# One DMA instead of two to spread the relative-bias rows over 128 scratch lines

## The chip, the cores and the metric

The kernel runs on one core of a Trainium2 chip. The metric is device time in microseconds (us) of one execution, the median of several. The same program is launched once; nothing is computed on the host.

## The reference, cut to what matters

Two blocks run one after the other on 256 tokens of width 1024. The first has two layers: layer 0 with a gated linear attention beside a sparse attention, then a dense SwiGLU; layer 1 with a forgetting and a dilated attention, then eight SwiGLU experts. The second block has one layer with an attention, a convolution and a SwiGLU. Three of these attentions add a bias that depends only on the distance between query and key:

```python
# layer 0 (sparse attention), rel_table: (32 buckets, 8 heads)
bias = rel_table[_rel_bucket(tq[None, :, None] - sel)]
logits = logits + bias.transpose(0, 3, 1, 2).astype(jnp.float32)
# layer 1 (dilated attention)
bias = rel_table[_rel_bucket(offs)].T.astype(jnp.float32)
lg = (jnp.einsum('bqhd,bqjhd->bhqj', qb, ksel) * dh ** -0.5 + bias[None, :, None, :])
# second block, rel_bias: (32, 8)
s_own = s_own + bias_ht[:, t5_bucket(jnp.maximum(dist_own, 0))]
```

## The kernel before, in words

**The bias tables.** For each of the three attentions the kernel first makes one row per head: 8 heads (on 8 partitions) by 384 distances, so 1.5 KB per partition. PE makes it with a one-hot product (L828, L829) and ACT copies it from PSUM into `relrow`, which lies in the tile `u` (L1275). What the attention adds is a table of 128 queries by 8 heads by 256 keys in which each query's line is the row shifted by one place. The shift is made by addressing: the rows are written 128 times into a scratch tensor in DRAM (`rel_dram`, named `rel_scratch` in the profile, 3 x 128 x 8 x 384 floats, 1.5 MB for each attention), and `bias_table` (L1977 to L1980) reads that with a pitch that is one element short, so that partition t gets the row from place 127 - t on. Its result is the tile `bias` (1 MB).

**How the scratch is written before.** POOL first stores the three small rows to a DRAM tensor `rel_rows` (L2014, 12 KB each), waits until all three have landed (L2015), then issues three DRAM-to-DRAM DMAs that each write 128 copies (L2017), and then `bias_table(0)`, which waits for the first of the three alone. Later `bias_table(1)` and `bias_table(2)` wait for theirs.

**POOL's queue around it** is a fixed order: norm weights, the steps above, `bias_table(0)`, the `rstd` of the gated linear attention (L1985), and, when the first attention has given its result, `bias_table(1)`. A wait in this queue holds everything behind it.

**Who depends on it.** DVE waits on `rel_out`, counted to 48, at L1749, because the next instructions overwrite `u` (L1753); at L1761 it waits for `rel_in[0]`, the bias table of the first attention, before the first add at L1597.

**The weights.** SP streams all weights in units of 1 MB into a ring of six (L411). ACT rounds each unit to its upper part (L1130, `upper`), DVE forms the rest (L1500, `lower`), and the end of DVE's instruction frees the place in the ring, so SP issues the load for the unit that is used six units later. PE takes three products for each pair of tiles (L524, L526, L527). In layer 0 each unit of 256 columns is one projection of q, k, v and so on; the sparse attention (L612 to L644) is threaded between the last of them. All DMAs, SP's and POOL's, are served by the same 16 DMA engines; queue q1 in the profile is SP's, q0 is POOL's.

Of the kernel before, what the change touches and what calls it, by code (L numbers as in the profile page):

```python
# [18 lines left out]
F32 = mybir.dt.float32  # L19
# [7 lines left out]
P = 128  # L27
# [4 lines left out]
H = 8  # L32
# [11 lines left out]
REL = 384  # L44
# [66 lines left out]
def build(nc, x_in, ln_g, ln_b, rel_table, w_in_ab, w_gate_a, b_gate_a, g_norm_a, w_out_ab, w_in_cd,  # L111
# [5 lines left out]
    with ctx:  # L117
# [3 lines left out]
        def sem(name):  # L121
            return ctx.enter_context(nc.semaphore(name))
# [59 lines left out]
            return psum[:, 2 * (i % 2):2 * (i % 2) + 2, 0:n]  # L182


        rel_rows = nc.dram_tensor("rel_rows", (3, H, REL), F32, kind="Internal").ap()
        rel_dram = nc.dram_tensor("rel_scratch", (3, P, H, REL), F32, kind="Internal").ap()


# [2 lines left out]
        relrow = uf[0:8, 2 * REL:5 * REL].rearrange("p (a n) -> p a n", a=3)  # L191
# [73 lines left out]
        ln_in = sem("norm_weights")  # L265
        late_in = sem("late_constants")
        rel_out = sem("rel_rows_out")
        rel_spread = [sem(f"rel_rows_spread_{i}") for i in range(3)]
        rel_in = [sem(f"rel_bias_in_{i}") for i in range(3)]
        rel_ready = sem("rel_row_ready")  # L270
        tr_done = sem("transposed")
# [1202 lines left out]
        def _(dve):  # L1474
# [20 lines left out]
            def lower():  # L1495

                u_, _, i, n = halves.place()
                s_ = halves.s
                dve.wait_ge(hi_ready[s_], n + 1)
                dve.tensor_tensor(lower_half[i], ring[:, u_, :], upper_half[i].bitcast(F32), ALU.subtract)\  # L1500
                   .then_inc(taken[s_][u_], 1)
# [467 lines left out]
        @block.gpsimd  # L1969
        def _(pool):  # L1970
            def weights(n, rows):
                if n >= 1:
                    pool.wait_ge(x_ready, n)
                for i, r in enumerate(rows):
                    pool.dma_start(lnw[:, i, :], r.broadcast_to([P, D])).then_inc(ln_in, 16)

            def bias_table(i):  # L1977
                pool.wait_ge(rel_spread[i], 16)
                src = bass.AP(rel_dram.tensor, i * P * H * REL + P - 1, [[H * REL - 1, P], [REL, H], [1, T]])
                pool.dma_start(bias[:, :, :], src).then_inc(rel_in[i], 16)  # L1980

            def rstd_of(n):
                asked[0] += 1
                pool.wait_ge(rs_ask, asked[0])
                pool.tensor_tensor(rstd8[:, 0:n], e2[:, 0:n], half[:, 0:n], ALU.pow).then_inc(rs_got, 1)  # L1985

            def rstd_tiles():
                for t in range(TT):
                    asked[0] += 1
                    pool.wait_ge(rs_ask, asked[0])  # L1990
                    pool.tensor_tensor(rstd8[:, t:t + 1], e2[:, t:t + 1], half[:, 0:1], ALU.pow).then_inc(rs_got, 1)

            halves = Split()

            def lower(s_, n):

                halves.at(s_, n)
                u_, _, i, n = halves.place()
                pool.wait_ge(hi_ready[s_], n + 1)
                pool.tensor_tensor(lower_half[i], ring[:, u_, :], upper_half[i].bitcast(F32), ALU.subtract)\  # L2000
                    .then_inc(taken[s_][u_], 1)

            def link(ins):
                chain[0] += 1
                ins.then_inc(g_chain, 1)
                pool.wait_ge(g_chain, chain[0])

            chain = [0]
            asked = [0]
            weights(0, (ln_g[0, 0:1, :], ln_b[0, 0:1, :]))  # L2010

            for i in range(3):
                pool.wait_ge(step_evac, 7 + i)
                pool.dma_start(rel_rows[i], relrow[:, i, :]).then_inc(rel_out, 16)  # L2014
            pool.wait_ge(rel_out, 48)  # L2015
            for i in range(3):
                pool.dma_start(rel_dram[i], rel_rows[i].unsqueeze(0).broadcast_to([P, H, REL])).then_inc(rel_spread[i], 16)  # L2017
            bias_table(0)
            pool.wait_ge(filled, 3)
            rstd_of(8)  # L2020
            pool.wait_ge(a_done, 2)
            bias_table(1)
            lower(0, 18)
            rstd_tiles()
            weights(1, (ln_g[0, 1:2, :], ln_b[0, 1:2, :]))
            pool.dma_start(rowsel[:, :, :], c_rowsel).then_inc(late_in, 16)
            lower(0, 18 + 3 * NCH_D)
            rstd_tiles()
            weights(2, (ln_g[1, 0:1, :], ln_b[1, 0:1, :]))
            pool.wait_ge(a_done, 6)  # L2030
            bias_table(2)
            pool.wait_ge(late_in, 16)
            pool.dma_start(convw[0:31, :], conv_w_2[0]).then_inc(late_in, 16)
            pool.dma_start(convw[31:32, :], conv_b_2).then_inc(late_in, 16)
            pool.dma_start(convg[:, :], conv_ln_g_2.broadcast_to([P, 512])).then_inc(late_in, 16)
            pool.dma_start(convb[:, :], conv_ln_b_2.broadcast_to([P, 512])).then_inc(late_in, 16)
            lower(0, LENGTHS[0])
            rstd_tiles()
            weights(3, (ln_g[1, 1:2, :], ln_b[1, 1:2, :]))
            pool.dma_start(mixg, mix_norm_g_2.broadcast_to([P, D])).then_inc(ln_in, 16)  # L2040
            rstd_tiles()
            rstd_tiles()
            weights(5, (ffn_norm_g_2,))

            rstd_of(2)
            lower(1, 11)
            rstd_tiles()
            weights(6, (final_norm_g_2.rearrange("(a d) -> a d", a=1),))
            rstd_tiles()
# [57 lines left out]
```

## Time and profile before

| | us |
|---|---|
| median of 3 runs (lowest, highest) | 1989.35 (1987.8, 1989.61) |
| the profiled execution | 1987.8 |
| its span, first to last instruction | 1985.7 |
| PE busy | 1871.4 (94%) |
| DVE busy | 1373.9 (69%) |
| ACT busy | 1110.0 (56%) |
| POOL busy | 50.5 (3%) |
| DMA: moved, mean rate | 490.43 MB, 247 GB/s |

The profiled execution lasts 2.1 us longer than its span and is the fastest of the three. Times inside the trace count from the span's start. Nearly all of the span is the stream of expert weights through PE; the change concerns the first tenth of it, in which the rows are made at 44 us, the scratch is written until 69 us and the first attention runs from 130 to 184 us.

### The profile page before, as it was taken

To read this page: it belongs to the slowest core of one execution; us is meant where nothing else is said; L and a number is where in the kernel's file an instruction comes from. 1 tells how busy PE (TensorE), PEld (TensorE's weight loads), DVE (VectorE), ACT (ScalarE), POOL (GpSimd) and SP (SyncE) were. 2 spreads that over 40 slices of the span, in tenths; PEclk is the share of its full clock that TensorE was granted. 3 is DMA by queue.
4 is the path that set the end of the run, shared out by engine and by line. 5 is a ranking of instruction groups with operands and counts; after the bars stand their busy time and mean duration, and the time that the engine had idled before them with its cause. 6 is when DMAs were issued, how large, how long until landed. Compare 5 with 4: busy or idle time off the path is not lost.

```text
span 1985.7 us, 26183 instructions
## 1 busy us (share of the span) xinstructions
PE 1871.4 (94%) x10221; PEld 1590.4 (80%) x10221; DVE 1373.9 (69%) x1207; ACT 1110.0 (56%) x1031; POOL 50.5 (3%) x49
## 2 busy tenths in 40 slices
PE   6999899989979999999999999999999978779998
PEld 5896799968967878878888788787887858669997
DVE  3742545453467888888888788888888875955544
ACT  4532343443436767677777777777767743334343
POOL 0000100010020000000000000000000000010000
PEclk9996899988979999999999999999999988789999
DMA  9631555542357999999999899998999972324551
GB/s 283 223 128 43 171 185 179 186 149 86 123 173 258 371 323 355 347 324 373 337 338 369 308 369 343 334 370 312 359 342 336 370 265 79 124 64 163 187 190 43
DMA packets 252154, 490.43 MB, mean 247 GB/s; under 512 B 14178, under 2 KB 96651, under 8 KB 251716
## 3 DMA queue, kind: packets, MB, share of 16 engines
q1 hardware_dynamic: 248144, 474.74, 68.3%
q0 software_dynamic: 3184, 14.29, 2.1%
q8 instruction: 38, 0.62, 0.1%
q10 hardware_dynamic: 772, 0.65, 0.1%
q14 instruction: 16, 0.13, 0.0%
HBM read 488.56 MB, written 5.80 MB: 249 GB/s over the span
## 4 chain that ended last, share of the span: by engine, by line
PE 87%; DVE 8%; issue 2%; ACT 2%; SPq 1%; DMA 1%; POOLq 0%; DVEq 0%; POOL 0%; ACTq 0%
PE psum L524 26%; PE psum L526 25%; PE psum L527 25%; DVE ta L1937 2%; PE psum L965 2%; PE psum L1037 2%; PE psum L1011 1%; DVE wl L1500 1%; ACT wh L1130 1%; PE psum L585 1%; PE psum L670 1%; PE psum L644 1%; PE psum L612 1%; DVE u L1881 1%; PE psum L697 1%
## 5 line engine op out<-in xcount | busy, mean ns | idle before, releaser
L1500 DVE TENSOR_TENSOR wl<-ring,wh 128x2048 fp32r<-128x2048 f32 x446 | 1021.9, 2291 | 406.2 <-ACT wh L1130 405.8
L1130 ACT ACTIVATE wh<-ring 128x2048 fp32r<-128x2048 f32 x450 | 861.6, 1915 | 428.1 <-PE psum L524 354.9
L524 PE MATMUL psum<-wh,xTh 128*128 128x512 f32 (+1 forms) x1168 | 447.4, 383 | 7.1 <-DVE wl L1500 3.1
L526 PE MATMUL psum<-wl,xTh 128*128 128x512 f32 (+1 forms) x1168 | 437.4, 375 | 0.0
L527 PE MATMUL psum<-wh,xTl 128*128 128x512 f32 (+1 forms) x1168 | 437.3, 374 | 0.0
L524 PE MATMUL psum<-xTh,wh 128*128 128x256 f32 x1088 | 314.0, 289 | 7.4 <-DVE wl L1500 4.8
L526 PE MATMUL psum<-xTl,wh 128*128 128x256 f32 x1088 | 311.8, 287 | 0.0
L527 PE MATMUL psum<-xTh,wl 128*128 128x256 f32 x1088 | 311.4, 286 | 0.0
L524 PEld LDWEIGHTS psum<-wh,xTh 128*128 128x128 f32 x1168 | 221.0, 189 | 49.3 <-issue 10.9
L527 PEld LDWEIGHTS psum<-wh,xTl 128*128 128x128 f32 x1168 | 220.6, 189 | 41.0
L526 PEld LDWEIGHTS psum<-wl,xTh 128*128 128x128 f32 x1168 | 221.1, 189 | 39.9 <-issue 1.9
L524 PE MATMUL psum<-wh,wnh 128*128 128x512 f32 x640 | 252.6, 395 | 0.0
L526 PE MATMUL psum<-wl,wnh 128*128 128x512 f32 x640 | 251.1, 392 | 0.0
L527 PE MATMUL psum<-wh,wnl 128*128 128x512 f32 x640 | 250.5, 391 | 0.0
L524 PEld LDWEIGHTS psum<-xTh,wh 128*128 128x128 f32 x1088 | 212.7, 196 | 10.5 <-issue 5.3
L526 PEld LDWEIGHTS psum<-xTl,wh 128*128 128x128 f32 x1088 | 212.9, 196 | 0.7
L527 PEld LDWEIGHTS psum<-xTh,wl 128*128 128x128 f32 x1088 | 212.7, 196 | 0.0
L527 PEld LDWEIGHTS psum<-wh,wnl 128*128 128x128 f32 x640 | 120.2, 188 | 26.5
L524 PEld LDWEIGHTS psum<-wh,wnh 128*128 128x128 f32 x640 | 120.3, 188 | 25.7 <-issue 0.6
L526 PEld LDWEIGHTS psum<-wl,wnh 128*128 128x128 f32 x640 | 120.3, 188 | 24.4
L1222 ACT ACTIVATE tk<-psum 128x256 f32<-128x256 f32 x44 | 17.0, 385 | 72.4 <-PE psum L527 72.4
L1398 ACT ACTIVATE tk<-psum 128x512 f32<-128x512 f32 x56 | 33.5, 599 | 32.6 <-PE psum L527 32.5
(260 smaller groups left out, 1225.2 us busy)
## 6 DMA issues: line engine op xcount, KB each, us to landing
ring<-in_w_moe SPq DMA_DIRECT2D x336, 1024.0 KB, 5.1
ring<-in_w_dense SPq DMA_DIRECT2D x33, 1024.0 KB, 5.2
ring<-in_w_in_ab SPq DMA_DIRECT2D x14, 1024.0 KB, 10.5
ring<-in_w_in_cd SPq DMA_DIRECT2D x12, 1024.0 KB, 5.2
ring<-in_w_gate SPq DMA_DIRECT2D x11, 1024.0 KB, 5.3
ring<-in_w_up SPq DMA_DIRECT2D x11, 1024.0 KB, 5.2
ring<-in_w_down SPq DMA_DIRECT2D x11, 1024.0 KB, 5.0
ring<-in_w_in SPq DMA_DIRECT2D x10, 1024.0 KB, 5.8
```

The source lines that it names most:

```text
L524: last = pe.matmul(o, a[0], b_[0], start=first, stop=False)
L526: pe.matmul(o, a[0], b_[1], start=False, stop=False)
L527: return pe.matmul(o, a[1], b_[0], start=False, stop=final)
L585: last = pe.transpose(bank[k // 2][:, (k % 2) * T + t * P:(k % 2) * T + (t + 1) * P], src[:, t, k * P:(k + 1) * P], ident[:, :])
L612: last = pe.matmul(o, q[rows, hp, t * P:(t + 1) * P], k[rows, hp, 0:n], start=True, stop=not more)
L644: last = pe.matmul(bank[4 + t][:, h * HD:(h + 1) * HD], pT[:, g % 2, (2 * hh + s) * P:(2 * hh + s + 1) * P], v[:, s, h * HD:(h + 1) * HD], ...
L965: last = pe.matmul(bank[6 + k // 4][:, (k % 4) * P:(k % 4 + 1) * P], x[:, t, k * P:(k + 1) * P], disp[:, t, :], start=(t == 0), stop=(t == 1))
L1037: last = pe.matmul(bank[(6, 2)[t] + h_][:, :], dispT[:, t * P:(t + 1) * P], y[:, 0, h_ * 512:(h_ + 1) * 512], start=True, stop=True)
L1130: act.activation(upper_half[i], ring[:, u_, :], ACT.Copy).then_inc(hi_ready[s_], 1)
L1398: act.activation(mh, bank[0][:, :], ACT.Silu).then_inc(m_silu, 1)
L1500: dve.tensor_tensor(lower_half[i], ring[:, u_, :], upper_half[i].bitcast(F32), ALU.subtract)\
L1937: last = dve.scalar_tensor_tensor(ta[:, c, :], upad[:, c, j:j + T], cw[:, c, j:j + 1], ta[:, c, :], ALU.mult, ALU.add)
```

## The change

The three DMAs of 12 KB to `rel_rows` and the three from `rel_rows` to the scratch become three DMAs that read the rows in SBUF 128 times and write the scratch directly. The tensor `rel_rows` and the semaphores `rel_spread` go. `rel_out` now counts the landing of the whole spread: POOL waits for all three before `bias_table(0)`, and DVE's wait on the same count at L1749 now stands for them too.

```diff
-        rel_rows = nc.dram_tensor("rel_rows", (3, H, REL), F32, kind="Internal").ap()
         rel_dram = nc.dram_tensor("rel_scratch", (3, P, H, REL), F32, kind="Internal").ap()
...
-        rel_spread = [sem(f"rel_rows_spread_{i}") for i in range(3)]
...
             def bias_table(i):
-                pool.wait_ge(rel_spread[i], 16)
                 src = bass.AP(rel_dram.tensor, i * P * H * REL + P - 1, [[H * REL - 1, P], [REL, H], [1, T]])
                 pool.dma_start(bias[:, :, :], src).then_inc(rel_in[i], 16)
...
             for i in range(3):
                 pool.wait_ge(step_evac, 7 + i)
-                pool.dma_start(rel_rows[i], relrow[:, i, :]).then_inc(rel_out, 16)
+                pool.dma_start(rel_dram[i].rearrange("t h j -> h t j"),
+                               relrow[:, i, :].unsqueeze(1).broadcast_to([H, P, REL])).then_inc(rel_out, 16)
             pool.wait_ge(rel_out, 48)
-            for i in range(3):
-                pool.dma_start(rel_dram[i], rel_rows[i].unsqueeze(0).broadcast_to([P, H, REL])).then_inc(rel_spread[i], 16)
             bias_table(0)
```

POOL's queue before, from the first of these DMAs to the second bias table (`rel_rows_out` is `rel_out`, `variance_ready` is what DVE gives when it asks for the `rstd`):

```order
L2014 DMA rel_rows<-u 8x384 [waits step_copied] x3
L2017 DMA rel_scratch<-rel_rows 128x3072 [waits rel_rows_out]
L2017 DMA rel_scratch<-rel_rows 128x3072 x2
L1980 DMA bias<-rel_scratch 128x8x256 [waits rel_rows_spread_0]
L1985 ISA
L1985 TENSOR_TENSOR rstd<-small,half 128x8 [waits variance_ready,fills_done]
L1980 DMA bias<-rel_scratch 128x8x256 [waits rel_rows_spread_1,heads_normed]
```

The same stretch of POOL's queue now (its line numbers are those of the changed kernel, L1982 is the `rstd`):

```order
L2011 DMA rel_scratch<-u 8x128x384 [waits step_copied] x3
L1977 DMA bias<-rel_scratch 128x8x256 [waits rel_rows_out]
L1982 ISA
L1982 TENSOR_TENSOR rstd<-small,half 128x8 [waits variance_ready,fills_done]
L1977 DMA bias<-rel_scratch 128x8x256 [waits heads_normed]
```

The scratch is now written by the first DMAs in the row, in the shape 8 x 128 x 384 with the head outermost, and the `rstd` stands behind the wait for all of them.

DVE's queue now, from the sixth `lower` before the first attention to the first bias add (in the kernel before it is the same row by row, with line numbers higher by two):

```order
L1498 TENSOR_TENSOR wl<-ring,wh 128x2048 [waits upper_halves_0,vector_chain]
L1746 TENSOR_SCALAR small<-small 128x8
L1750 TENSOR_TENSOR nr<-nr,rstd 128x512 [waits rel_rows_out,rstd_ready]
L1751 TENSOR_TENSOR u<-nr,psum 128x512 [waits vector_chain]
L1750 TENSOR_TENSOR nr<-nr,rstd 128x512
L1751 TENSOR_TENSOR u<-nr,psum 128x512 [waits vector_chain]
L1498 TENSOR_TENSOR wl<-ring,wh 128x2048 [waits upper_halves_0] x2
L1595 TENSOR_TENSOR lg<-psum,bias 128x2x128 [waits scores_ready,rel_bias_in_0]
```

Nothing moved on DVE; the semaphore in the third row now stands for the spread, and two `lower` instructions, hence two weight units, stand behind it.

## Rows read from the trace of the kernel before

**Rows 1.** The page: busy time of each engine, and the chain that ended last

```profile
PE 1871.4 (94%) x10221; PEld 1590.4 (80%) x10221; DVE 1373.9 (69%) x1207; ACT 1110.0 (56%) x1031; POOL 50.5 (3%) x49
PE 87%; DVE 8%; issue 2%; ACT 2%; SPq 1%; DMA 1%; POOLq 0%; DVEq 0%; POOL 0%; ACTq 0%
```

**Rows 2.** POOL's timeline: start, duration, engine, line, operation, count [idle before <-releaser]

```profile
44.86 1.03 POOL L2014 DMA_DIRECT2D rel_rows<-u  x2 [42.36 <-ACT u L1275]
48.15 0.50 POOL L2014 DMA_DIRECT2D rel_rows<-u  x1 [2.26 <-ACT u L1275]
50.12 1.58 POOL L2017 DMA_DIRECT2D rel_scratch<-rel_rows  x3 [1.47 <-DMA rel_rows<-u]
59.08 0.92 POOL L1980 DMA_DIRECT2D bias<-rel_scratch  x1 [7.37 <-DMA rel_scratch<-rel_rows]
122.81 1.68 POOL L1985 TENSOR_TENSOR rstd<-small,half 128x8 f32<-128x8 f32 x1 [62.81 <-DVE small L1748]
```

**Rows 3.** DVE's timeline around the waits for `rel_out` and the bias table

```profile
111.84 2.29 DVE L1500 TENSOR_TENSOR wl<-ring,wh 128x2048 fp32r<-128x2048 f32 x1 [6.53 <-ACT wh L1130]
120.28 2.29 DVE L1500 TENSOR_TENSOR wl<-ring,wh 128x2048 fp32r<-128x2048 f32 x1 [4.83 <-ACT wh L1130]
124.52 0.69 DVE L1752 TENSOR_TENSOR nr<-nr,rstd 128x512 f32<-128x512 f32 x1 [1.87 <-POOL rstd L1985]
127.18 2.29 DVE L1500 TENSOR_TENSOR wl<-ring,wh 128x2048 fp32r<-128x2048 f32 x1
134.68 0.42 DVE L1597 TENSOR_TENSOR lg<-psum,bias 128x256 f32<-128x256 f32 x1
```

**Rows 4.** DMA view, 48.1 to 50.2 us, the third 12 KB copy alone: 40 slices

```profile
GB/s 0 0 0 0 0 0 0 0 0 0 0 0 0 0 0 0 0 0 0 0 0 117 30 59 30 0 0 0 0 0 0 0 0 0 0 0 0 0 0 0
DMA packets 32, 0.01 MB, mean 6 GB/s; under 512 B 24, under 2 KB 32, under 8 KB 32
rel_rows<-u POOLq DMA_DIRECT2D x1, 12.0 KB, 1.7
```

**Rows 5.** DMA view, 50 to 67 us, the three spreads

```profile
q0 software_dynamic: 411, 4.64, 84.5%
```

**Rows 6.** DMA view, 183 to 190 us, a bias table alone

```profile
DMA packets 272, 1.05 MB, mean 150 GB/s; under 512 B 16, under 2 KB 16, under 8 KB 272
bias<-rel_scratch POOLq DMA_DIRECT2D x1, 1024.0 KB, 6.0
```

**Rows 7.** DMA view, 30 to 40 us, weight units alone

```profile
DMA packets 3443, 3.49 MB, mean 349 GB/s; under 512 B 48, under 2 KB 3442, under 8 KB 3442
```

**Rows 8.** SP's timeline: two loads of weight units

```profile
64.11 0.37 SPq L411 DMA_DIRECT2D ring<-in_w_in_ab  x1
72.65 0.37 SPq L411 DMA_DIRECT2D ring<-in_w_in_ab  x1
```

**Rows 9.** DMA view, 68 to 70 us, both queues busy

```profile
q0 software_dynamic: 151, 0.61, 81.0%
q1 hardware_dynamic: 94, 0.10, 17.8%
```

**Rows 10.** Instructions of line L411: landing for issues at 63 to 65, then 70 to 130

```profile
DMA to landing us min/median/max: 10.9/10.9/10.9
...
DMA to landing us min/median/max: 4.8/5.0/6.1
```

**Rows 11.** ACT's timeline: the upper parts of the units lowered at 111.84 and 120.28

```profile
109.83 1.90 ACT L1130 ACTIVATE wh<-ring 128x2048 fp32r<-128x2048 f32 x1
118.27 1.90 ACT L1130 ACTIVATE wh<-ring 128x2048 fp32r<-128x2048 f32 x1
123.54 0.60 ACT L1146 ACTIVATE tk<-psum 128x512 f32<-128x512 f32 x1 [3.37 <-PE psum L527]
```

**Rows 12.** PE's timeline: the first attention scores, and the projection after them

```profile
129.94 0.48 PE L612 MATMUL psum<-tk,tq 64*128 64x128 f32 x2 [0.69 <-ACT tk L1146]
133.10 0.36 PE L524 MATMUL psum<-wh,xTh 128*128 128x256 f32 x1
```

## Prediction, made before the changed kernel was run

> **What bounds the kernel now.** I read the page first: PE is busy 94% of the span and 87% of the chain that ended last is PE, POOL is busy 3% [rows 1]. So POOL's work costs nothing by itself; it matters only if PE, or what feeds PE, comes to wait for it. I went next to POOL's timeline, to see when the edited DMAs run [rows 2], and to DVE's timeline, to see when their result is wanted [rows 3]. The reader sees a large gap between the two. The scratch writes are issued at 50.1 us and the first bias table at 59.1 us. DVE wants `rel_out` and the `rstd` at 122.6 us (it begins again at 124.52, after 1.87 us of waiting for POOL), and the bias table at 134.68 us. The DMA view of those writes came next [rows 5], and last the weight loads, because they use the same 16 DMA engines [rows 7 to 11].
>
> In this stretch weights are not short. SP issues a load when DVE frees a place, the unit is used six units later, and the load issued at 64.11 is the one that ACT rounds at 109.83 and DVE lowers at 111.84 [rows 3, 8, 11]. It lands after 10.9 us, later ones after about 5 [rows 10]: some 35 us of cover each.
>
> **What the change removes.** Three DMAs of 12 KB and one wait of 1.47 us for their landing, and three issues of 0.53 us (1.58 in all) at 50.12 [rows 2]. They ended 60 us before anybody asked, so their going is worth 0. On POOL three issues stay, with 1024 runs each instead of 8; the bias table's issue has 1024 runs too and takes 0.92 us [rows 2], so POOL pays about 1.2 us more, also hidden (POOL then idles until 122.8).
>
> **What it adds: where the bytes are read.** The spread still writes 3 x 128 x 12,288 B = 4.72 MB, but reads them from 8 SBUF partitions instead of DRAM, in runs of 1.5 KB instead of 12 KB. How fast 8 partitions can be read is the unknown of this case. The upper bound is the rate of the full set of engines in the spreads before: 4.64 MB in 84.5% of 16 engines over 17 us is 20.2 GB/s for each engine, 323 GB/s for sixteen [rows 5], so 15 us. The lower bound: if the rate goes by partition, 8 of 128 partitions get a sixteenth of the 349 GB/s at which weight units fill all 128 [rows 7], 21.8 GB/s, and the spread takes 216 us. The nearest row by far is the third 12 KB copy, which runs alone and reads these same 8 partitions in runs of 1.5 KB: 32 packets, of which 8 carry data, and all of it lies in four slices of 52.5 ns [rows 4]. That is 12.3 KB in 0.21 us, 58.5 GB/s. It is short, so pipelining flatters it and start-up hurts it. I take it: 4.72 MB / 58.5 GB/s = 81 us.
>
> A rule of the Trainium skill speaks against this change in the same sense. The page SBUF — State Buffer, section "Door 1: The DMA port swizzle", says that partitions 0 to 3 sit behind one of 16 DMA ports and 4 to 7 behind another, each good for about 27.2 GB/s. No row here shows a port by itself; rows 4 agree in size. An estimate from that page, 54.4 GB/s for two ports, would make the spread 87 us and, by the steps below, the whole 18 us slower instead of 12.
>
> **When the spread is done.** The first DMA is issued at 44.86. The third 12 KB copy was issued at 48.15, moved its first packet at 49.22 (1.07 us later) and landed 1.7 us after its issue, some 0.4 us after its last packet [rows 2, 4]. So bytes flow from 45.9 to 126.6 and `rel_out` is full at about T = 127.0.
>
> **First consequence, the constants.** POOL waits for T, issues the bias table (0.92 us) and makes the `rstd` (1.68 us) [rows 2]: 129.6 against 124.5, 5.1 us late. Queued behind it on DVE are 2.7 us of scaling and the two `lower` that start at 127.18 and 132.47 [rows 3]. PE wants the first of these only at 133.10 [rows 12], and it was done at 129.47: slack of 3.6 us. By this way alone the end moves by 1.5 us. The bias table, issued at T, lands 6.0 us after issue when alone [rows 6], at 133 to 137; the first add would stand at about 137 to 140 anyway. No further cost.
>
> **Second consequence, the weights.** While the spread lies in the 16 engines, weight packets share them. With both queues full, 151 packets of q0 and 94 of q1 went in 2 us [rows 9], so each engine takes about one from each in turn, not bytes in proportion. A weight unit is 1024 packets of 1 KB (3443 packets for 3.49 MB, [rows 7]), 64 for each engine. A bias table of 1024 runs goes in 272 less 16 packets [rows 6], four runs of 1 KB each; so I take two runs of 1.5 KB in a packet of the spread, 1536 packets, 96 for each engine, one every 81 / 96 = 0.84 us. Then the unit issued at 64.11 needs 64 x 0.84 = 54 us from about 65.6 on, to 119.5, where ACT wants it at 109.83. The next one, issued at 72.65, gets what is left until T, some 9 packets for each engine, and the other 55 after it: 2.7 us at the rate of rows 7, plus about 1.5 us for the bias table that now shares the engines. It is there at about 131, and ACT wants it at 118.27 [rows 11]: 12.7 us late. Its slack on PE is 0.9 us: its lower part was done at 122.57, and the projection ahead of it ended at 123.54, when ACT took that one's result [rows 3, 11]. Everything behind it moves by 12.7 - 0.9 = 11.8 us: PE's scores from 129.94 to 141.7 [rows 12], and in that shadow the 5.1 us of the constants disappears, since both act on the same chain. Later units are already queued in SP's row and land 3 us apart, faster than the 5.8 us in which PE uses one. Nothing behind gives the time back: what follows is a chain of norm, dense layer and experts in which PE is the bound.
>
> **Sum.** Removed 0, POOL's issues 0, constants 1.5 (within the next), weights 11.8: +12 us. The profiled execution would go from 1987.8 to 1999.8, its span from 1985.7 to 1997.5. It lies 1.55 us below the median of the runs, so the median goes from 1989.35 to 2001.
>
> **The rivals.**
> *A. The read is no bottleneck: no change.* If 8 partitions feed the engines as fast as DRAM did (20.2 GB/s each [rows 5]), the first two spreads on eight engines each take 9.7 us and the third 9.7 more: T = 66, the bias table lands before 80, 55 us before its add. Time 1989. For it: [rows 4] is one tiny copy, in whose first slice alone 117 GB/s are seen. Against it: the same row's mean. The point from which it decides: the second weight unit must be there by 118, and 1 MB after T takes 3 to 4 us, so T must be under about 114, which is 4.72 MB in 68 us, 69 GB/s. Above that the change costs nothing.
> *B. The spread is slow but weights slip past it.* While engines wait on SBUF for one queue they may move packets of the other. Then only the constants are late: T = 127 gives +1.5, T = 133 gives 7.5. Time 1991 to 1997. For it: [rows 9] has q1 moving well with q0 present. Against it: the unit issued at 64.11 landed after 10.9 us instead of 5, with q0 ahead of it [rows 10].
> *C. The rate goes by partition.* 216 us at 21.8 GB/s, T = 262. The second unit then arrives at about 266 where 118.27 was wanted, +147 us, time 2136. Against it: [rows 4], nearly three times that rate.
> *D. Faster.* Only if the 10.9 us landing at 64 had held somebody up; its user had 35 us to spare. About 0.
>
> **How the numbers follow.** The forecast (slow read, weights late) gets 0.52, A 0.28, B 0.12, C 0.07, D 0.01. The time is the forecast's, 2001; its own range, by rates from 65 down to 48 GB/s, is 1993 to 2020. The range for 8 in 10 takes in A and B below and stops short of C: 1988 to 2024. About 0.2% (4 us) is what a measurement of this kernel can tell from no change. Slower by more than that: most of the forecast (0.49), C, and the later half of B (0.08 with what is rounded): 0.64. Faster: 0.03, for the spread between runs. Same: 0.33.
>
> **What would show it.** In the changed profile the landing of the three spreads should be about 80 us after issue, with q0 moving some 50 to 60 GB/s from 46 to 127 us; POOL's bias table should be issued at about 127 and no longer at 59; ACT's rounding at 109.83 and 118.27 should wait for the DMA of the ring, the second by 12 us; the chain should pass through that landing. The forecast is wrong if the spreads land before 114; A then holds. If they land late and the units on time, B holds and DVE's idle time ends on POOL's `rstd`. If PE's delay at the first scores is given back later, my last step is wrong.

## The result and the profile after

The changed kernel is slower: 2017.13 us (median of 4; 2014.1 to 2018.16) against 1988.57 us of the kernel before on the same chip. The ratio is 1.0142, 95% interval 1.0125 to 1.016, so 25 to 32 us. The forecast was 2001 in a range of 1988 to 2024: the right way, but 12 us where 28.6 were measured. The profiled execution of the changed kernel took 2011.46 us (span 2009.7) and is the fastest of its five; its span is 24.0 us over that of before.

POOL's timeline of the changed kernel answers to [rows 2]; L2011 is the new spread, L1977 the bias table, L1982 the `rstd`.

```profile
47.00 2.22 POOL L2011 DMA_DIRECT2D rel_scratch<-u  x2 [44.50 <-ACT u L1273]
50.29 1.06 POOL L2011 DMA_DIRECT2D rel_scratch<-u  x1 [1.07 <-ACT u L1273]
144.53 0.93 POOL L1977 DMA_DIRECT2D bias<-rel_scratch  x1 [93.17 <-DMA rel_scratch<-u]
150.15 1.68 POOL L1982 TENSOR_TENSOR rstd<-small,half 128x8 f32<-128x8 f32 x1 [4.69 <-DVE small L1746]
```

The spread is over at 144.5 us, not at 127 as forecast. But POOL then waits another 4.69 us for DVE: the `rstd` was not late, its caller was. DVE's timeline, which answers to [rows 3], shows it; the wait for POOL is 1.87 us, exactly what it was before.

```profile
136.04 2.29 DVE L1498 TENSOR_TENSOR wl<-ring,wh 128x2048 fp32r<-128x2048 f32 x1 [6.04 <-ACT wh L1128]
147.62 2.29 DVE L1498 TENSOR_TENSOR wl<-ring,wh 128x2048 fp32r<-128x2048 f32 x1 [7.98 <-ACT wh L1128]
151.87 0.69 DVE L1750 TENSOR_TENSOR nr<-nr,rstd 128x512 f32<-128x512 f32 x1 [1.87 <-POOL rstd L1982]
162.96 0.42 DVE L1595 TENSOR_TENSOR lg<-psum,bias 128x256 f32<-128x256 f32 x1
```

So time was lost before these rows. The wait view of the changed kernel from 45 to 180 us says where (columns: who waits, for whom, us in total, times, longest):

```profile
PEld psum L525 <- issue: 19.0, 2, 9.6
PE psum L525 <- issue: 9.4, 1, 9.4
PE psum L524 <- issue: 9.3, 1, 9.3
ACT wh L1128 <- DMA ring<-in_w_in_ab: 3.0, 1, 3.0
DVE nr L1750 <- POOL rstd L1982: 1.9, 1, 1.9
```

"Issue" means that the engine waited for nothing that another engine gives. PE stands still twice, in the middle of a row of identical products of one weight unit, with no wait for data. PE's timeline at the two places:

```profile
83.31 0.37 PE L524 MATMUL psum<-wl,xTh 128*128 128x256 f32 x1 [9.32 <-issue]
...
110.89 0.58 PE L525 MATMUL psum<-wh,xTl 128*128 128x256 f32 x1 [9.43 <-issue]
```

What PE lacks, as I read it, is the next piece of its own program. The DMA view of the changed kernel from 66 to 86 us shows one transfer on the instruction queue in 20 us; taken 2 us at a time it lies between 80 and 82, just before PE goes on at 83.3 (the other gap ends at 110.9, with one between 108 and 110). In the kernel before the corresponding transfer, the first after one at 30 us in both kernels, goes at 57.9 us, 12 us before PE reaches this product at 70.0; the first row below is from there (view of the kernel before, 57 to 59 us), the other three are the changed kernel's from 66 to 86.

```profile
q8 instruction: 1, 0.02, 2.9%
DMA packets 226, 1.05 MB, mean 53 GB/s; under 512 B 0, under 2 KB 0, under 8 KB 225
q0 software_dynamic: 225, 1.04, 96.1%
q8 instruction: 1, 0.02, 0.3%
```

That it is the program and not chance, two things in the traces bear out. The two gaps open before the 347th and the 474th matmul of PE, 257 instructions of PE apart in the trace (matmuls and weight loads), and the gaps of runs 6 and 10 below open before the same two; the one gap of run 4 lies 256 further on. And in all seven of them PE goes on 2.2 to 2.4 us after a transfer of 16 KB has started on the instruction queue.

The rows for 66 to 86 us also give the rate of the spread, 1.04 MB in 20 us or 52 GB/s, with all 16 engines 96% busy at it, and its packets: 4.6 KB, three runs each, an engine's time 20 x 16 x 0.96 / 225 = 1.37 us. After each gap PE also runs slow for some 5 us. The table of stretches (busy us of PE, PEld, DVE, ACT, POOL; granted clock, DMA share, GB/s):

```profile
73.00:84.00 11.00, 1.68 (x13) 1.58 (x12) 7.57 (x23) 0.00 (x0) 0.00 (x0) 0.75 0.96 53
84.00:88.00 4.00, 4.00 (x21) 4.00 (x21) 0.00 (x0) 0.17 (x1) 0.00 (x0) 0.50 0.94 51
88.00:92.00 4.00, 4.00 (x32) 4.00 (x32) 1.67 (x1) 3.97 (x5) 0.00 (x0) 0.90 0.98 53
```

PE was idle for most of 11 us, and the granted clock stood at 0.50 (1.2 GHz of 2.4) while it began again: 21 products where the stretch after has 32.

A ledger over the projections, by the moment at which ACT takes each result (L1146 before, L1144 after):

| result | before | after | later by | what came in between |
|---|---|---|---|---|
| queries of the linear attention (`tb`) | 59.36 | 63.19 | 3.8 | 2.1 of it before the first changed DMA |
| values (`nw`) | 72.65 | 87.83 | 15.2 | first gap, 9.3, and the slow clock |
| gate (`nr`), second | 92.25 | 117.90 | 25.7 | second gap, 9.4, and the slow clock |
| keys (`tk`), first | 123.54 | 147.74 | 24.2 | 1.5 comes back; not followed up |
| keys (`tk`), second | 129.29 | 157.57 | 28.3 | weight unit late, 3.03 on ACT |

Two gaps make 11.4 + 10.5 = 21.9 us, the late unit 4.1 us. The first 3.8 us are not shown to be the change's; runs of unchanged speed start this stretch up to 2.3 us later as well (47.12 for 44.86 in the run with one direct spread below), and run 1 is 1.4 us later than the kernel before by the place of the first gap.

From the first attention on both kernels do the same work, but the distance still moves, as the starts of the same matmul in both traces show: 28.3 us at the second keys, 32.2 at 227 us of the kernel before, 27.2 at 502, 24.7 at 704 and 24.0 at the end. The 3.9 us lost are not shown to be the change's: run 1 loses 2.5 there against the same trace. Of the 8.2 us that come back, 5 do so in layer 1, where PE's granted clock was 0.97 against 0.93 in the trace before. The trace of run 10, where the same three slow spreads run, shows 0.93 there, gives nothing back after 227 us and ends 31.3 us later than before.

### The profile page after: what moved, and what is told of

The parts are those of the page before. It is cut to its first block, busy times and chain, and to the rows that moved or that the text cites. A ratio compares the mean times of both kernels' runs of the same rounds, so it can differ in the third digit from the quotient of the medians.

```text
span 2009.7 us, 26178 instructions
## 1 busy us (share of the span) xinstructions
PE 1873.5 (93%) x10221; PEld 1594.5 (79%) x10221; DVE 1374.1 (68%) x1207; ACT 1110.2 (55%) x1031; POOL 50.7 (3%) x46
## 4 chain that ended last, share of the span: by engine, by line
PE 86%; DVE 7%; issue 3%; ACT 2%; SPq 1%; DMA 1%; another core or an unknown queue 0%; POOLq 0%; DVEq 0%; POOL 0%; ACTq 0%
PE psum L522 25%; PE psum L524 25%; PE psum L525 25%; DVE ta L1935 2%; PE psum L963 2%; PE psum L1035 2%; PE psum L1009 1%; ACT wh L1128 1%; DVE wl L1498 1%; PE psum L668 1%; PE psum L583 1%; PE psum L610 1%; PE psum L642 1%; PE psum L615 1%; DVE u L1879 1%
```

## The experiments

Lines that appear in the diffs are against the changed kernel, where nothing else is said. "Before" in each is the kernel before on the same chip.

**1. What sets the rate of the spread: how many partitions are read.** The rows are made on all 128 partitions and all are read.

```diff
+        rel = sb("rel", [32, 2, 16, H])          # each table 16 times, by a broadcast load
+                pe.matmul(ps[0:P, 0:REL], rel[:, w, :, :].rearrange("p r h -> p (r h)"), onehot[:, w, :], ...)
+                pool.dma_start(rel_dram[i].rearrange("(s r) h j -> (r h) s j", r=16),
+                               relrow[0:128, i, :].unsqueeze(1).broadcast_to([128, 8, REL])).then_inc(rel_out, 16)
```

> The rows are made on all 128 partitions (sixteen copies of the eight heads, by sixteen times as many columns in the same product), and the three spreads read all 128 partitions, each run of 1.5 KB eight times instead of 128. Bytes, runs, writes, POOL's queue and all waits are those of the changed kernel. Theory R (the read of eight neighbouring SBUF partitions sets the rate): the spread ends at about 47 + 1 + 4.72 MB / 323 GB/s = 63 us, 70 at most, and the time is that of the kernel before, 1989 within 4 us. Rival D (the cost lies in 1.5 KB runs, in scattered writes to DRAM, or in the descriptors of GpSimd's queue): the spread still takes 80 us or more and the time stays near 2015.

Measured: 1986.91 us against 1987.33, ratio 0.9995 (0.9983 to 1.0006). The bias table is issued at 61.54 us instead of 144.53. With the same bytes, runs, queue and waits the loss is gone, so this run's rival D (not the prediction's) fell: neither 1.5 KB runs nor, with a quick spread, the waits cost anything.

**2. Eight partitions again, but apart.** The rows are made as in run 1.

```diff
-                               relrow[:, i, :].unsqueeze(1).broadcast_to([H, P, REL])).then_inc(rel_out, 16)
+                               relrow[0:64:9, i, :].unsqueeze(1).broadcast_to([H, P, REL])).then_inc(rel_out, 16)
```

> As the run before, but the spreads read only eight partitions again, now 0, 9, 18, ... 63, one for each head, instead of 0 to 7. Same number of partitions, of engines, of runs and of repeats as in the changed kernel. Theory N (neighbouring partitions share one way out): eight engines at up to 20 GB/s each move it in 25 to 35 us, the spread ends between 70 and 85 us and the time is 1989 within 5 us. Rival S (each partition has a rate of its own, 52 GB/s / 8 = 6.5 GB/s): 91 us as in the changed kernel, end at about 140, time 2015. Rival K (what is slow is that only eight engines take part): also 91 us.

Measured: 1990.91 against 1987.33, ratio 1.0021 (1.0011 to 1.0031). POOL's timelines of runs 1 and 2:

```profile
61.54 0.89 POOL L1977 DMA_DIRECT2D bias<-rel_scratch  x1 [12.28 <-DMA rel_scratch<-u]
```

```profile
73.33 0.94 POOL L1977 DMA_DIRECT2D bias<-rel_scratch  x1 [23.79 <-DMA rel_scratch<-u]
```

Eight partitions that lie nine apart give 4.72 MB in 27 us (46.1 to 73.3), 173 GB/s; eight neighbours give 52 (49 over the whole spread, 48.1 to 144.5 us). Rivals S and K fell. Neighbours share one way out. This is what the Trainium skill says (SBUF — State Buffer, "Door 1: The DMA port swizzle"): partitions 0 to 3 and 4 to 7 sit behind one port each, while the eight read here sit behind eight. The 0.2% that remain (0.1 to 0.3) are at the limit of what can be measured; I did not look for their cause.

**3. The new waits alone.** Against the kernel before:

```diff
+            for i in range(3):
+                pool.wait_ge(rel_spread[i], 16)
             bias_table(0)
```

and the same three waits for DVE at L1749.

> The kernel before, with its two-step spread, but with the waits of the changed one: POOL waits for all three spreads before the first bias table, and DVE waits for all three before it overwrites u. In the kernel before the last spread lands at 69 us and DVE asks at 122.5, so both theories that follow expect no change, 1989 within 3 us; if it is slower, the new waits cost something by themselves, which no step of the prediction has.

Measured: 1984.95 against 1987.33, ratio 0.9992 (0.9979 to 1.0004). The waits cost nothing while the spread is quick (bias table issued at 69.44).

**4. The slow traffic alone.** Against the kernel before, with the source a constant that is never overwritten:

```diff
             bias_table(0)
+            for i in range(3):
+                pool.dma_start(rel_extra[i].rearrange("t h j -> h t j"),
+                               cumf[0:8, 0:REL].unsqueeze(1).broadcast_to([H, P, REL])).then_inc(extra_out, 16)
```

> The kernel before plus three more DMAs of the slow kind (8 neighbouring partitions of the constant tile cum, 128 times 1.5 KB each, to a scratch of their own), issued behind the first bias table at 59 us, waited for only at the end. Nobody needs them, so constants and bias tables are on time. They should drain from 60 to about 151. Theory T (the slow packets in the 16 engines hold up other transfers: weight units and the loads of PE's instructions): +20 to +35 us, 2009 to 2024, with PE idle for 9 us at a time on issue and ACT waiting for the ring. Rival C (only those who wait for the spread itself lose): no change, 1989.

Measured: 2026.01 against 1987.33, ratio 1.0186 (1.0169 to 1.0203). This run's rival C (not the prediction's) fell: nobody waits for these bytes, and they cost more than the change does, 2 us more even than theory T allowed. The wait view of this run, 42 to 220 us (its L1133 is `upper`, L1503 `lower`, L527 and L530 PE's products):

```profile
ACT wh L1133 <- DMA ring<-in_w_in_ab: 45.9, 3, 26.8
PE psum L527 <- DVE wl L1503: 35.9, 5, 22.9
PE psum L530 <- issue: 5.8, 1, 5.8
```

Here it is the weight units: they land 46 to 88 us after their issue, against 5 to 11 before, and PE waits 35.9 us for them and only 5.8 us on issue. The slow packets start later in PE's program than in the changed kernel: POOL's queue first moves the spreads from DRAM and the bias table, and the rate falls to some 60 GB/s only at 74 us (in the changed kernel at 49.5). By then the two instruction transfers that come late in the changed kernel have gone, at 58.1 and 70.8 us; the one behind them goes at 109.2, just before PE's only gap on issue ends at 111.4. So the same packets met mostly the other victim.

**5 and 6. One and two of the three spreads by the new way**, the rest by `rel_rows` as before. Against the kernel before, with k = 1 and k = 2 (the waits on DVE and POOL are changed to match):

```diff
-                pool.dma_start(rel_rows[i], relrow[:, i, :]).then_inc(rel_out, 16)
+                if i < k:
+                    pool.dma_start(rel_dram[i].rearrange("t h j -> h t j"),
+                                   relrow[:, i, :].unsqueeze(1).broadcast_to([H, P, REL])).then_inc(rel_spread[i], 16)
+                else:
+                    pool.dma_start(rel_rows[i], relrow[:, i, :]).then_inc(rel_out, 16)
```

> One spread of three by the new way, the other two by rel_rows as before. The slow one should drain by about 47 + 31 = 80 us if it has the eight partitions to itself, on eight engines. Theory W (the time is set by when the spread is over: a weight unit or a constant is then wanted and not there, from 114 us on): no loss, 1989 within 3. Theory I (PE's instruction loads stand behind slow packets whenever PE needs the next piece of its program, at about 73 us in the changed kernel): +8 to +12 us with a PE gap on issue near 70 us, 1997 to 2001.

> Two spreads of three by the new way. They should drain by about 47 + 62 = 110 us on all 16 engines. Theory W: still inside the cover of the weights (limit 114), at most +3 us, 1989 to 1992. Theory I: both gaps of PE on issue (73 and 101 us) are there: +18 to +24 us, 2007 to 2013.

Measured: with one, 1985.19 against 1987.98, ratio 0.999 (0.998 to 1.0); with two, 2002.62 against 1987.98, ratio 1.0081 (1.0063 to 1.0099). With two the spreads are over at 114.4 us, ACT never waits for the ring, and PE's timeline has both gaps:

```profile
83.66 0.37 PE L526 MATMUL psum<-wl,xTh 128*128 128x256 f32 x1 [12.31 <-issue]
...
110.99 0.58 PE L527 MATMUL psum<-wh,xTl 128*128 128x256 f32 x1 [9.19 <-issue]
```

This is PE's instruction load by itself: theory W, which allowed 3 us at most, fell as the only cause; theory I was right on the gaps and high on the time (15 to 16 us against 18 to 24). The limit of 114 us under rival A of the prediction, before which a slow spread was to cost nothing, fell too: both direct spreads are over at 114.4 and the time is lost all the same. With one spread it is theory I, as I had put it, that fell: no gap, although the slow packets run from 48 to 81 us. The DMA view of that run, 60 to 80 us, has the difference:

```profile
q0 software_dynamic: 245, 1.01, 47.2%
q1 hardware_dynamic: 1053, 1.06, 17.6%
```

One spread draws the same 50 GB/s but holds 47.2% of the engines' time, which I read as half of the engines, each packet of 4.6 KB for 0.69 us, and a weight unit still lands in that window. Two hold all 16.

**7. Sixteen neighbouring partitions.**

```diff
+                pool.dma_start(rel_dram[i].rearrange("(s r) h j -> (r h) s j", r=2),
+                               relrow[0:16, i, :].unsqueeze(1).broadcast_to([16, 64, REL])).then_inc(rel_out, 16)
```

The rows are made as in run 1.

> Rows on 16 neighbouring partitions, spreads read partitions 0 to 15, all else as in the changed kernel. If neighbours share a way out by groups, the rate doubles to about 105 GB/s: the spread takes 45 us and ends at about 94 us. Theory W: no loss, 1989 within 3. Theory I: one gap of PE, about half as long, since each packet takes half the time: +4 to +8 us, 1993 to 1997. If the rate stays at 52 GB/s although 16 partitions and 16 engines take part, the way out is wider than groups of eight and the time stays near 2015.

Measured: 1989.08 against 1987.98, ratio 1.0003 (0.9992 to 1.0014). The DMA view, 60 to 80 us:

```profile
DMA packets 528, 2.10 MB, mean 105 GB/s; under 512 B 32, under 2 KB 93, under 8 KB 526
q0 software_dynamic: 497, 2.04, 96.8%
```

The rate is 102 GB/s, double that of eight, as expected; the bias table is issued at 96.44. All 16 engines are 97% held at it, each packet of 4.6 KB for 0.70 us (20 x 16 x 0.968 us by 2.04 MB / 4.6 KB), and PE has no gap, where theory I had expected one. The instruction transfer has the reason; this is its row in the same run, 66 to 68 us:

```profile
q8 instruction: 1, 0.02, 2.9%
```

It goes at 67.4 us, 3.9 us before PE reaches the product of the first gap; in the kernel before it went 12 us ahead, in the changed kernel (81.1) it goes 7 us after PE has run dry at 74.0. So it is not that the engines are full, but how long the others' turn takes: behind packets of 1.37 us PE's load comes too late, behind packets of 0.70 us late, but in time. The run halves the packets' time by doubling the rate; that the one matters and not the other is not shown.

**8. One slow DMA more, wanted by nobody.** Run 4 with `range(1)`.

> The kernel before plus one DMA of the slow kind (1.57 MB from 8 partitions of cum), issued behind the first bias table at 59 us; nobody waits for it. It drains from 60 to about 92 us on eight engines. Theory W: no loss, since no weight unit is late by more than its cover of 35 us: 1989 within 3. Theory I: PE's instruction load at 73 us stands behind slow packets: +8 to +12 us, unless it is served by the eight engines that are free.

Measured: 1987.89 against 1987.98, ratio 1.0006 (0.9996 to 1.0017); it landed 41.3 us after issue and PE had no gap. It agrees with run 5.

**9. The three spreads issued by ACT**, and POOL's three taken out:

```diff
                 act.activation(relrow[:, i, :], step_out()[0:8, 0:REL], ACT.Copy).then_inc(step_evac, 1)
+                act.wait_ge(step_evac, 7 + i)
+                act.dma_start(rel_dram[i].rearrange("t h j -> h t j"),
+                              relrow[:, i, :].unsqueeze(1).broadcast_to([H, P, REL])).then_inc(rel_out, 16)
```

> The changed kernel with one thing moved: ACT issues the three spreads, right behind the copies that make the rows, in place of POOL. Bytes, runs, source partitions and waits on rel_out stay. In all traces so far transfers of ACT and SP go in packets of one run each (1 KB), those of POOL in packets of several (4.6 KB in the changed kernel, 1.4 us of an engine each). Theory P (what others lose is their turn behind such a long packet, PE's instruction load first): packets are now 1.5 KB and take a third, so PE has no gap on issue over 3 us; the spread still takes 90 us (end near 138), and since it still holds the engines, weight units are what comes late: 3 to 20 us lost, 1992 to 2008. Rival B (what others lose is proportional to how many bytes wait ahead of them, whatever the packets): PE's two gaps of 9 us stay, 2015 or more. Rival R (the slow rate itself came from POOL's descriptors): the spread ends before 80 us and the time is 1989.

Measured: 2025.35 against 1988.64, ratio 1.0182 (1.0165 to 1.0199). No expectation had the cause, which ACT's queue shows:

```profile
44.88 0.30 ACTq L1275 DMA_DIRECT2D rel_scratch<-u  x1
45.73 10.38 ACTq L1275 DMA_DIRECT2D rel_scratch<-u  x1
56.66 31.63 ACTq L1275 DMA_DIRECT2D rel_scratch<-u  x1
```

The issue itself holds ACT for 31.63 us (until earlier packets have gone, I take it; that is not shown), and PE waits 40.0 us for the scores that ACT should take. The time is above the range of theory P. The run still says two things. The spread is over at 145.0, the same rate, so R fell: GpSimd's queue is not what makes it slow. And PE has no gap of 9 us on issue (the longest after the scores is 1.1). Packets are now single runs of 1.5 KB and all three spreads together keep the engines 44.9% busy (64 to 84 us), so I read them as lying on half of the engines:

```profile
q10 hardware_dynamic: 657, 1.00, 44.9%
```

Both favour PE's load at once, so the run does not tell which of them helped.

**10. An attempt to put all three on the same eight engines.** A 12 KB copy between the spreads (DVE and POOL wait for the copies too):

```diff
+                if i < 2:
+                    pool.dma_start(rel_rows[i], relrow[:, i, :]).then_inc(rel_small, 16)
```

> The changed kernel with a 12 KB copy of the same eight partitions to DRAM, on POOL's queue, between the spreads (24 KB more in all). If POOL's transfers of eight partitions take eight engines in turn, as the half-busy engines of the run with one such spread suggest, all three spreads now lie on the same eight engines and the other eight are free. The spread still takes about 90 us, end near 138. Theory P: only half as many engines draw on the slow read, so a packet takes 0.7 us instead of 1.4 and PE's instruction load is late by under 3 us, if at all; weight units use all engines, the units wanted at 118 and 123 us come near 140: +15 to +30 us, 2004 to 2018, and ACT waits for the ring. Rival B (bytes ahead count): the queue on those eight is as long as both were, gaps of PE as in the changed kernel and 2015 or more. If the time is 1989, weight units were never what mattered.

Measured: 2009.09 against 1988.64, ratio 1.0096 (1.0079 to 1.0113). The edit missed its aim: q0 holds 97.0% of 16 engines from 64 to 84 us, so the copy does not shift the choice of engines. What is left is a second look at the changed kernel: gaps of 11.5 and 9.8 us, end of the spread at 145.05. Its median lies 20 us over that of the kernel before, where the changed kernel lies 28.6 over; its four executions spread from 2005.5 to 2018.9, and what makes the difference stays open.

## Why the prediction was wrong

**What bounds the kernel: right.** POOL's own work cost nothing; the loss came by way of what feeds PE.

**The rate: right in kind, 11% off.** I took 58.5 GB/s from a copy of 0.21 us [rows 4]; it is 52. With a start 2.1 us later and a third spread that runs alone at about 45 GB/s on half of the engines (0.82 MB from 126 to 144 us), the end came at 144.5 instead of 127.0. The estimate by the port figure of the Trainium skill (SBUF — State Buffer, "Door 1: The DMA port swizzle"; 54.4 GB/s, 87 us) was nearer than my row.

**The constants: no part in it.** I had 1.5 us, inside the next term. The `rstd` and the bias table (landed by 154.4, wanted at 162.96) were in time, because DVE was later still. Run 3 shows the waits are free when the spread is quick; in the changed kernel this is read from the trace, not shown by a run.

**The weights: the step that was mis-sized, twice over.** I let each engine take one packet of each queue in turn, every 0.84 us. The turns are as I had them, once both queues move: the DMA view of the changed kernel, 96 to 106 us, has

```profile
q0 software_dynamic: 110, 0.51, 94.8%
q1 hardware_dynamic: 109, 0.11, 3.1%
```

But the spread's packets carry three runs, not two, and last 1.37 us. And my term left out the wait for the first turn: the unit issued at 67.93 moved its first packet at 91.0, 23 us or 17 packets of the spread later (23.4 in run 6, 24.2 in run 10, 13.5 in run 7 with its quicker packets, 1.1 in run 5). The term still came out near, by luck: the rest of that unit went quickly once two spreads had landed at 110 and 113 us, and it was there 53.2 us after its issue, where I had 54. The next took 69.1 us and was the late one, at 145.6. Yet it cost 4.1 us and not 11.8, since PE, delayed elsewhere, came for it later. Run 4 shows what the units cost where PE is not delayed first: 35.9 us of PE's time.

**What was missing: PE's instruction load.** The sum counted the tensors that share the 16 engines and left out the program. The step that failed is "Second consequence, the weights" as the one thing that comes late on PE's path. The instruction load sets out behind the same slow packets as the weight unit did: it goes 23.2 us later than in the kernel before (81.1 for 57.9), though PE is only 3.8 us later by then. The two gaps with the slow clock behind them are 21.9 of the 28.3 us at the second keys. Run 6 shows them without any late unit. [Rows 1] had "issue 2%" on the chain, and I did not ask what it was.

**"Nothing behind gives the time back": only in part.** In the trace of run 10 the delay stays; in the profiled executions of the changed kernel and of run 6 about 8 us come back behind the first attention, at a higher granted clock than in the trace before.

**Rivals.** A and C fell by the rate, B (weights slip past) by the landings, D by the sign. None of them had this victim. The own range, 1993 to 2020, held the time by the luck of two errors of opposite sign. The prediction's own sum with the measured end of the spread, T = 144.5 instead of 127.0, makes 11.8 + 17.5 = 29.3 us, close to the 28.6; that is luck too, since it puts all of it on late weights, and they cost 4.1.

That the two victims add up to no more than one of them when they overlap is argued from runs 4 and 6 and from the ledger; no run took the instruction load away and left the units late.

## What to carry to other kernels

A transfer that nobody waits for can still stop the engine that matters, if it is slow at its source: count how many of the DMA engines it holds and how long each of its packets holds one, not its bytes. List everything that shares those engines, and put the instruction loads of a long unrolled stretch on the list beside the tensors. Where a small tile must be read many times by DMA, lay copies of it over all partitions first (here one product with 128 columns instead of 8, at no cost), or read partitions that lie far apart.

## What the runs showed of the hardware

- Reading SBUF by DMA in runs of 1.5 KB: partitions 0 to 7 give 52 GB/s and 0 to 15 give 102, both in a window of 20 us; over the whole spread eight partitions nine apart give 173, all 128 about 305 (4.72 MB from 46 to 61.5 us).
- One DMA from eight neighbouring partitions keeps the 16 engines 47.2% busy, two of them 96.1%; a packet of 4.6 KB then lasts 0.69 and 1.37 us.
- Behind two such DMAs a queue that was idle gets its first packet 23 to 24 us after the issue (weight loads of the changed kernel, runs 6 and 10), and then one packet for one (109 to 110).
- PE stops when its next instructions come late: 9.2 to 12.3 us at a time where two slow DMAs were in flight, and the granted clock is 0.50 for about 5 us afterwards.
- Issuing can block: ACT's third spread held ACT for 31.63 us. SP shows it in the changed kernel too; the issues of its weight loads from 45 to 180 us, which take 368 ns at best, reach 27.8 us:

```profile
L409 SPq DMA_DIRECT2D ring<-in_w_in_ab x5: 368/597/27824, 44.9 to 114.9; - x5
```
